# A two-block transformer kernel on one core: where the split of the next weight piece stands among the head steps of the gate tiles

## The chip, the cores and the metric

The kernel runs on one core of a Trainium2 chip. The metric is the device time of one execution in microseconds (us), of which less is better.

## What is computed

Two networks run one after the other on a sequence of 256 tokens of width 1024, in fp32. The first has two layers (windowed and neighbourhood attention with memory heads, gated feed-forward). The second, where the change lies, has one block:

```python
proj = jnp.dot(xn, w_in[l]) + b_in[l]
q, k, v, qi, ki, wi, xr, yr, gate_a, gate_b = jnp.split(proj, cuts, axis=-1)
attn = dsa_attention(...)            # 8 heads, keys chosen by a top-k of index scores
xr = causal_dwconv(xr, conv_rnn_w[l], conv_rnn_b[l])
rnn = rg_lru(xr, ...) * jax.nn.gelu(yr)
merged = (jax.nn.sigmoid(gate_a) * jnp.dot(attn, w_o_attn[l])
          + jax.nn.sigmoid(gate_b) * jnp.dot(rnn, w_o_rnn[l]))
h = h + ga1 * jnp.dot(merged, w_out[l])
```

## The kernel before

Every large product is done in three matmuls of type fp32r: activations and weights are each split into a high part (rounded to that type) and a low part (what is left), and high x high, high x low and low x high are summed in PSUM (L901 to L903). The weights come from memory in pieces of 128 partitions x 2048 numbers. For piece m, SP loads it into one of four raw buffers; ScalarE copies it to the high buffer `hi` (L1219), for which it waits until TensorE is done with piece m - 3 (`part_done`, three buffers); VectorE subtracts to get `lo` (L1663), and this subtraction lets TensorE use the piece and SP overwrite the raw buffer (the load of the piece four further on). These two instructions together are the step called the *split* of piece m.

The class `Order` writes one list of steps before the program is built, and each engine runs its own instructions of each step in the order of that list. So on every engine the order of the list is the order of the work, and an instruction that waits holds all that stands behind it on its engine. A *tile* of output columns (512 wide) takes two pieces, and the 24 matmuls of a piece are cut into two chunks of 12. `Order.part` (from L362) puts a chunk (`mm`), then, after a piece's first chunk, the split of the piece three further on, and between chunks it calls `between`, which takes the next entry of the tile's list in `IN2` (L35) or pops tasks that wait in `later`:

```python
            self.steps.append(("mm", m, ch))
            if ch == 0 and not self.hold:
                self.split_through(self.owed)
            if ch < p.chunks - 1:
                between()
```

The tiles of the second block's input projection are, in order: xr, qi, kvw, xr, yr, yr, q, then the two tiles of gate b (`gb`, pieces 112 to 115), the two of gate a (`ga`, 116 to 119), and then the recurrence's output projection (`orn`, 120 to 123). After them come `oat` (124, 125) and `out2`. In the gaps between their chunks stand, in order:

- gb: `gate1..` (the recurrence's two gates of half 1: TensorE matmuls, ScalarE Sigmoid L1343), `q0`, `q2` (transposes of q, split into parts), `top4` to `top7` (rounds of the top-k on VectorE), `rec1` (ScalarE: a table load, four Exp, four Tanh, two squares L1360; VectorE L1831); then `mask` (VectorE, L1820 to L1824), `inc1` (ScalarE square root, GpSimd product L1995), `attend`, `scan1` (VectorE scan L1837, then the GpSimd product L2000 that ends the recurrence of half 1).
- ga: `bias1` (GpSimd loads the bias rows of heads 4 to 7), `half1` (ScalarE L1368, VectorE L1842: the recurrence's output is split), and the head steps `att 0` to `att 5`.
- orn: the head steps 6 to 14.

A head step `att i` works on several heads at once (`attention` in each engine's program): TensorE transposes the weights of head i - 3 (called P below, L877), computes the scores of heads i and i + 1 if i is even, and multiplies the weights of head i - 5 with the values (L976 to L978). VectorE adds bias and mask to the scores of head i - 1 with their minimum (L1486), takes the reciprocal of the sum of head i - 2 (L1447), and makes the low part of P of head i - 4 (L1425). ScalarE makes the high part of that P (L1101) and the two exponentials of head i - 1 (L1125, L1126). GpSimd scales head i - 2 (L1901, L1902) and adds the mask for head i + 1 (L1884). At the end of a gate tile VectorE adds the bias to both halves (L1609).

Of the kernel before, what the change touches and what calls it, by code (L numbers as in the profile page):

```python
# [114 lines left out]
class Part:  # L115


    def __init__(self, m, at, tile, source, first, last, k0, nk, w):
        self.m, self.at, self.tile, self.source, self.first, self.last = m, at, tile, source, first, last
        self.k0, self.nk, self.w = k0, nk, w  # L120
        self.chunks = (2 * nk + 3) // 4
        if tile.bank:
            self.chunks = 2
# [13 lines left out]
class Order:  # L137
# [3 lines left out]
    def __init__(self, plan):  # L141
        self.plan = plan
        self.weights = [i for i, p in enumerate(plan) if p[0] != "ada"]
        self.steps, self.later, self.made = [], deque(), set()
        self.parts, self.tiles = [], []
        self.turn_n, self.turn_at, self.taken = 0, {}, {ON_A: 0, ON_D: 0}
        self.idle, self.tenant, self.bank_at, self.before = deque(range(8)), [None] * 8, {}, {}
        self.ada_at, self.split_next, self.owed, self.hold = {}, 0, 0, False
        self.squares, self.square_n = {}, 0
        self.h2_at, self.h2_n, self.silu_at, self.prod_at = {}, 0, {}, {}  # L150
        self.conv_at, self.conv_slots, self.pending, self.multiplied = {}, [], deque(), deque()
        self.tile_of = {}
        self.summed_by = {}
        self.res_at = {}
        self.run()
        self.count()
# [205 lines left out]
    def part(self, tile, source, first, last, between):  # L362
        m = len(self.parts)
        i = self.weights[m]
        _, k0, nk, w = self.plan[i][1]
        p = Part(m, i, tile, source, first, last, k0, nk, w)
        self.parts.append(p)
        for ch in range(p.chunks):
            for k in range(8) if tile.bank else [k0 + n % nk for n in range(4 * ch, min(4 * ch + 4, 2 * nk))]:
                self.need((source, k))  # L370
            self.steps.append(("mm", m, ch))
            if ch == 0 and not self.hold:
                self.split_through(self.owed)
            if ch < p.chunks - 1:
                between()
        self.owed = m + SPLITS
        if last:
            tile.m = m
            if tile.bank:
                self.turn_at[tile.bank] = (None, None, None)  # L380
# [122 lines left out]
    def run(self):  # L503
        for k in range(0, 8, 2):
            self.put("memx", k)
            self.split_through(min(k // 2, SPLITS - 1))
        self.later.extend([("rows",), ("relload",), ("xin", 0, 0), ("xin", 0, 2), ("xin", 0, 4), ("xin", 0, 6), ("memsq",), ("sq", 0, 0), ("sq", 0, 1)])
        self.linear("mem", 0, 0, 512, len(FIRST), "mem", [2, 1, 1, 2])
        self.mix(0)
        self.later.append(("rpb",))  # L510
        self.later.append(("small",))
        self.ffn(0)
        self.mix(1)
        self.drain()
        self.put("adaprep")
        self.ffn(1)
        self.drain()
        self.put("park")
        self.put("roots12")
        self.modulated(0)  # L520
        self.put("block2")
        for what, c, w, between in IN2:
            self.linear("yr" if what == "yr" else "in2", what, c, w, 1 if w <= 256 else 2, ("z", 0), 0, between)
        for c in (0, 512):
            self.linear("orn", 2, c, 512, 2, "r", 2)
        self.drain()
        self.put("fetch")
        self.put("sigmoid_a")
        for c in (0, 512):
            self.linear("oat", 2, c, 512, 1, ("y", 2))  # L530
        for c in (0, 512):
            self.linear("out2", 2, c, 512, 2, "merged")
        self.drain()
        self.put("root2")
        self.modulated(1)
        for c, w in UP2:
            for what in ("gate", "value"):
                self.linear("raw", what, c, w, 1, ("z", 1))
        self.later.extend([("flush",), ("flush",)])
        for c in (0, 512):  # L540
            self.linear("down2", 2, c, 512, 6, "h2")
        self.drain()
        self.put("root3")
        self.put("end")
# [1612 lines left out]
```

## Time and profile before

| what | us |
|---|---|
| runs, median of 3 | 1064.32 (1063.88 to 1067.81) |
| the profiled execution's own time | 1068.08 |
| its span, first to last instruction | 1066.0 |
| TensorE busy | 1014.6 (95%) |
| VectorE busy | 728.1 (68%) |
| ScalarE busy | 567.8 (53%) |
| GpSimd busy | 114.9 (11%) |
| mean granted TensorE clock | 0.988 |

How to read it: the page gives busy times and shares over the whole span; the trace below it gives single instructions with start and duration. The times in the trace count from the start of the span; the profiled execution's own time is 2.1 us longer than its span. The stage of the change lies between about 732 and 820 us. Of the chain of work that ended last, TensorE holds 73% and VectorE 10%.

### The profile page before, as it was taken

Reading aid. Unit: us, or ns where it says so; the run is one execution under the profiler, and the core shown is the slowest. Engines: PE = TensorE matmul, PEld = TensorE weight load, DVE = VectorE, ACT = ScalarE, POOL = GpSimd, SP = SyncE. Lnnn points to the kernel's source line nnn. Section 1 sums busy time; section 2 is a strip of 40 time slices with the busy share of each in tenths; the row PEclk is TensorE's granted clock in tenths of the full one; section 3 lists DMA queues with packets and bytes.
Section 4 is the critical chain, followed back from the end, with each engine's and each line's share of the span. In section 5 each row is a group of like instructions: output and inputs, shape, how many; then the busy total and the mean of one; then the engine's idle time right before and its main releaser. Section 6 shows DMA issues by size and latency. Waiting matters only on the chain.

```text
span 1066.0 us, 14098 instructions
## 1 busy us (share of the span) xinstructions
PE 1014.6 (95%) x5524; PEld 859.5 (81%) x5524; DVE 728.1 (68%) x984; ACT 567.8 (53%) x816; POOL 114.9 (11%) x167
## 2 busy tenths in 40 slices
PE   6998999999999989899999999999979999999996
PEld 5776777889888877788888877888867789999885
DVE  5668775566356568568878676688875767777753
ACT  6657654444345567544344435586656456565541
POOL 0112140000000022200000001122530000000001
PEclk9999999999999999999999998999999999999999
DMA  9765489655556431379999896555555436555541
GB/s 349 281 171 77 145 210 292 198 183 178 187 188 197 158 119 52 108 264 355 336 339 327 311 338 212 178 168 198 175 184 184 159 100 223 173 198 171 166 138 39
DMA packets 107376, 214.02 MB, mean 201 GB/s; under 512 B 4400, under 2 KB 32320, under 8 KB 103920
## 3 DMA queue, kind: packets, MB, share of 16 engines
q1 hardware_dynamic: 102640, 196.39, 54.5%
q0 software_dynamic: 4384, 16.51, 6.5%
q8 instruction: 44, 0.72, 0.3%
q10 hardware_dynamic: 288, 0.23, 0.1%
q14 instruction: 20, 0.16, 0.0%
HBM read 208.39 MB, written 6.15 MB: 201 GB/s over the span
## 4 chain that ended last, share of the span: by engine, by line
PE 73%; DVE 10%; ACT 7%; DMA 4%; issue 4%; POOL 1%; DVEq 0%; SPq 0%; ACTq 0%; POOLq 0%
PE bank L901 18%; PE bank L903 18%; PE bank L902 18%; PE bank L918 4%; PE bank L920 4%; PE bank L919 4%; ACT hi L1219 4%; DVE lo L1663 3%; PE bank L877 3%; DMA raw<-in_w_gate_up 3%; ACT junk L1089 1%; PE bank L930 1%; DMA raw<-in_w_in_a 1%; PE bank L879 1%; DVE early L1486 1%
## 5 line engine op out<-in xcount | busy, mean ns | idle before, releaser
L1663 DVE TENSOR_TENSOR lo<-raw,hi 128x2048 fp32r<-128x2048 f32 (+2 forms) x164 | 364.8, 2227 | 220.6 <-ACT hi L1219 220.2
L1219 ACT ACTIVATE hi<-raw 128x2048 fp32r<-128x2048 f32 (+2 forms) x164 | 303.6, 1855 | 243.3 <-PE bank L903 138.1
L901 PE MATMUL bank<-hi,xTh 128*128 128x512 f32 (+2 forms) x688 | 268.8, 391 | 1.2 <-DVE lo L1663 1.2
L903 PE MATMUL bank<-hi,xTl 128*128 128x512 f32 (+2 forms) x688 | 262.6, 382 | 0.0
L902 PE MATMUL bank<-lo,xTh 128*128 128x512 f32 (+2 forms) x688 | 262.2, 381 | 0.0
L901 PEld LDWEIGHTS bank<-hi,xTh 128*128 128x128 f32 x688 | 131.0, 190 | 26.1 <-DVE lo L1663 1.6
L903 PEld LDWEIGHTS bank<-hi,xTl 128*128 128x128 f32 x688 | 130.6, 190 | 25.2
L902 PEld LDWEIGHTS bank<-lo,xTh 128*128 128x128 f32 x688 | 130.9, 190 | 22.8
L901 PE MATMUL bank<-hi,hTh 128*128 128x512 f32 x264 | 103.3, 391 | 0.2 <-DVE lo L1663 0.2
L902 PE MATMUL bank<-lo,hTh 128*128 128x512 f32 x264 | 102.8, 389 | 0.0
L903 PE MATMUL bank<-hi,hTl 128*128 128x512 f32 x264 | 102.8, 389 | 0.0
L918 PE MATMUL bank<-xTh,hi 128*128 128x256 f32 x352 | 99.9, 284 | 1.7 <-DVE lo L1663 1.0
L919 PE MATMUL bank<-xTh,lo 128*128 128x256 f32 x352 | 99.6, 283 | 0.0
L920 PE MATMUL bank<-xTl,hi 128*128 128x256 f32 x352 | 99.6, 283 | 0.0
L918 PEld LDWEIGHTS bank<-xTh,hi 128*128 128x128 f32 x352 | 67.5, 192 | 2.3 <-DVE lo L1663 1.2
L919 PEld LDWEIGHTS bank<-xTh,lo 128*128 128x128 f32 x352 | 67.6, 192 | 0.0
L920 PEld LDWEIGHTS bank<-xTl,hi 128*128 128x128 f32 x352 | 67.6, 192 | 0.0
L901 PEld LDWEIGHTS bank<-hi,hTh 128*128 128x128 f32 x264 | 49.6, 188 | 10.7 <-DVE lo L1663 0.6
L903 PEld LDWEIGHTS bank<-hi,hTl 128*128 128x128 f32 x264 | 49.6, 188 | 10.3
L902 PEld LDWEIGHTS bank<-lo,hTh 128*128 128x128 f32 x264 | 49.6, 188 | 10.1
L1675 DVE SCALAR_TENSOR_TENSOR big<-raw,small,big 128x2048 f32<-128x2048 f32 x24 | 56.3, 2344 | 0.0
L1653 DVE SCALAR_TENSOR_TENSOR big<-bank,cols,big 128x255 f32<-128x255 f32 (+2 forms) x100 | 41.1, 473 | 3.4 <-ACT big L1325 2.8
(360 smaller groups left out, 1386.4 us busy)
## 6 DMA issues: line engine op xcount, KB each, us to landing
raw<-in_w_gate_up SPq DMA_DIRECT2D x44, 1024.0 KB, 7.2
raw<-in_w_down SPq DMA_DIRECT2D x30, 1024.0 KB, 5.1
raw<-in_w_ada SPq DMA_DIRECT2D x24, 1024.0 KB, 7.1
raw<-in_w_up SPq DMA_DIRECT2D x22, 1024.0 KB, 5.1
raw<-in_w_in SPq DMA_DIRECT2D x20, 1024.0 KB, 5.3
raw<-in_w_out SPq DMA_DIRECT2D x12, 1024.0 KB, 5.1
raw<-in_w_in_b SPq DMA_DIRECT2D x10, 1024.0 KB, 5.1
raw<-in_w_in_a SPq DMA_DIRECT2D x6, 1024.0 KB, 11.8
```

The lines of the kernel that those rows point to most:

```text
L877: e.transpose(bank[:, i * 128:(i + 1) * 128], x, ident)
L879: e.transpose(bank[:, n * 128:(n + 1) * 128], blocks[n], ident).then_inc(x_full, 1)
L901: e.matmul(o, sh, h[:, k, :], start=p.first and k == 0, stop=False)
L902: e.matmul(o, sh, lo[:, k, :], start=False, stop=False)
L903: done = e.matmul(o, sl, h[:, k, :], start=False, stop=p.last and k == p.nk - 1)
L918: e.matmul(o, h[:, k, at], xh[:, k, :], start=k == 0, stop=False)
L919: e.matmul(o, lo[:, k, at], xh[:, k, :], start=False, stop=False)
L920: done = e.matmul(o, h[:, k, at], xl[:, k, :], start=False, stop=k == 7)
L1219: e.activation(hi_s[m % SPLITS][:, 0:n], raw[p.at % RAWS][:, 0:n], ACT.Copy).then_inc(hi_made, 1)
L1653: e.scalar_tensor_tensor(out=o[:, j, n:], in0=bank[:, j * 256:j * 256 + 256 - n], scalar=weights[j][n - 1], in1=o[:, j, n:], op0=ALU.mult, ...
L1663: e.tensor_tensor(lo_s[s][:, 0:n], raw[p.at % RAWS][:, 0:n], hi_s[s][:, 0:n].bitcast(F), ALU.subtract).then_inc(lo_made, 1)
L1675: e.scalar_tensor_tensor(out=piece, in0=raw[i % RAWS][:, :], scalar=small[:, k:k + 1], in1=piece, op0=ALU.mult, op1=ALU.add).then_inc(ada_ ...
```

## The change

In the tiles of gate b and gate a, and in orn after them, a chunk's hook steps (what `between` puts) stand ahead of the split of the next piece, not behind it. The flag stays on through orn, since it is cleared only after that. Eleven splits move, those of pieces 114 to 124; the twelfth, of piece 125, keeps its place, as no step is left to pop there.

```diff
--- before.py
+++ after.py
@@ -151,6 +151,7 @@
         self.conv_at, self.conv_slots, self.pending, self.multiplied = {}, [], deque(), deque()
         self.tile_of = {}
         self.summed_by = {}
+        self.hooks_first = False
         self.res_at = {}
         self.run()
         self.count()
@@ -369,9 +370,12 @@
             for k in range(8) if tile.bank else [k0 + n % nk for n in range(4 * ch, min(4 * ch + 4, 2 * nk))]:
                 self.need((source, k))
             self.steps.append(("mm", m, ch))
+            first = self.hooks_first
+            if first and ch < p.chunks - 1:
+                between()
             if ch == 0 and not self.hold:
                 self.split_through(self.owed)
-            if ch < p.chunks - 1:
+            if not first and ch < p.chunks - 1:
                 between()
         self.owed = m + SPLITS
         if last:
@@ -520,10 +524,12 @@
         self.modulated(0)
         self.put("block2")
         for what, c, w, between in IN2:
+            self.hooks_first = what in ("gb", "ga")
             self.linear("yr" if what == "yr" else "in2", what, c, w, 1 if w <= 256 else 2, ("z", 0), 0, between)
         for c in (0, 512):
             self.linear("orn", 2, c, 512, 2, "r", 2)
         self.drain()
+        self.hooks_first = False
         self.put("fetch")
         self.put("sigmoid_a")
         for c in (0, 512):
```

Nothing changes on TensorE, GpSimd and SP. ScalarE around the step rec 1, before (`hi1<-raw3` is the high half of piece 115, `hi2<-raw0` of 116, `hi0<-raw1` of 117, `hi1<-raw2` of 118; the Exp write `nrm`, the Tanh `big`, the squares a bank; line numbers of the kernel before):

```order
L1219 ACTIVATE hi1<-raw3 128x2048 [waits part_done,d_raw3]
L1206 ACTIVATE q2yh<-bank1 128x512 [waits x_full]
L1353 ACT_TABLE_LOAD [waits x_act,rate_made]
L1353 ACTIVATE nrm<-big,small 128x256 [waits ig_x]
L1353 ACTIVATE nrm<-big,small 128x256 x3
L1357 ACTIVATE big<-big,small 128x256 [waits decay_made]
L1357 ACTIVATE big<-big,small 128x256 x3
L1360 ACTIVATE bank2<-nrm 128x512 [waits x_act]
L1360 ACTIVATE bank0<-nrm 128x512 [waits x_act]
L1219 ACTIVATE hi2<-raw0 128x2048 [waits part_done,d_raw0]
L1364 ACT_TABLE_LOAD
L1364 ACTIVATE big<-big 128x1024 [waits mult_made]
```

and in the changed kernel (its line numbers are higher by 6):

```order
L1212 ACTIVATE q2yh<-bank1 128x512 [waits x_full]
L1359 ACT_TABLE_LOAD [waits x_act,rate_made]
L1359 ACTIVATE nrm<-big,small 128x256 [waits ig_x]
L1359 ACTIVATE nrm<-big,small 128x256 x3
L1363 ACTIVATE big<-big,small 128x256 [waits decay_made]
L1363 ACTIVATE big<-big,small 128x256 x3
L1366 ACTIVATE bank2<-nrm 128x512 [waits x_act]
L1366 ACTIVATE bank0<-nrm 128x512 [waits x_act]
L1225 ACTIVATE hi1<-raw3 128x2048 [waits part_done,d_raw3]
L1370 ACT_TABLE_LOAD
L1370 ACTIVATE big<-big 128x1024 [waits mult_made]
L1225 ACTIVATE hi2<-raw0 128x2048 [waits part_done,d_raw0]
```

The high half of piece 115 has gone from ahead of the second copy of q to behind the squares.

VectorE around the head steps 2 and 3, before (`lo2<-raw3` is piece 119, `lo0<-raw0` piece 120; `ISA` rows are the scores of one head; `nrm<-` rows the bias adds of the gate tile):

```order
L1663 TENSOR_TENSOR lo2<-raw3,hi2 128x2048 [waits hi_made]
L1486 ISA acc,stat1<-bank0,big 128x128 [waits masked,p_made,x_full]
L1486 ISA stat1 128x1
L1486 ISA acc,stat1<-bank0,big 128x256
L1486 ISA stat1 128x1
L1447 RECIPROCAL stat0<-stat0 128x2 [waits exp_made]
L1609 TENSOR_TENSOR nrm<-bank3,gbc 128x512 [waits acc_first,d_brow1,r_low]
L1609 TENSOR_TENSOR nrm<-bank1,gbc 128x512 [waits part_done]
L1663 TENSOR_TENSOR lo0<-raw0,hi0 128x2048 [waits hi_made]
L1486 ISA stage0,stat2<-bank4,big 128x128 [waits masked,p_made,x_full]
L1486 ISA stat2 128x1
```

and in the changed kernel:

```order
L1492 ISA acc,stat1<-bank0,big 128x128 [waits masked,p_made,x_full]
L1492 ISA stat1 128x1
L1492 ISA acc,stat1<-bank0,big 128x256
L1492 ISA stat1 128x1
L1453 RECIPROCAL stat0<-stat0 128x2 [waits exp_made]
L1669 TENSOR_TENSOR lo2<-raw3,hi2 128x2048 [waits hi_made]
L1615 TENSOR_TENSOR nrm<-bank3,gbc 128x512 [waits acc_first,d_brow1,r_low]
L1615 TENSOR_TENSOR nrm<-bank1,gbc 128x512 [waits part_done]
L1492 ISA stage0,stat2<-bank4,big 128x128 [waits masked,p_made,x_full]
```

The scores of head 1 and the reciprocal of head 0 (`stat0`) are now ahead of piece 119's subtraction. Further on, the same kind of place between head steps 3 and 4, in the changed kernel:

```order
L1492 ISA stat2 128x1
L1453 RECIPROCAL stat1<-stat1 128x2 [waits exp_made]
L1669 TENSOR_TENSOR lo0<-raw0,hi0 128x2048 [waits hi_made]
L1492 ISA stage0,stat3<-bank5,big 128x128 [waits masked,p_made,x_full]
L1492 ISA stat3 128x1
L1492 ISA stage0,stat3<-bank5,big 128x256
L1492 ISA stat3 128x1
L1453 RECIPROCAL stat2<-stat2 128x2 [waits exp_made]
L1431 TENSOR_TENSOR p2l0<-bank2,p2h0 128x384 [waits x_high]
```

The subtraction of piece 120 now stands between the reciprocal of head 1 and the scores of head 3; before, it stood ahead of head 2's scores, and those of head 3 followed the reciprocal of head 1 directly.

## Rows read from the trace of the kernel before

**Rows 1.** The page: busy time of each engine, and the clock in 40 slices.
```profile
PE 1014.6 (95%) x5524; PEld 859.5 (81%) x5524; DVE 728.1 (68%) x984; ACT 567.8 (53%) x816; POOL 114.9 (11%) x167
...
PEclk9999999999999999999999998999999999999999
```

**Rows 2.** TensorE's timeline, 752 to 808: start us, us, line, operation, [idle before <- releaser].
```profile
752.18 0.39 PE L901 MATMUL bank<-hi,xTh 128*128 128x512 f32 x1
...
777.43 0.44 PE L877 MATMUL bank<-const 128*128 128x128 f32 x2 [3.81 <-POOL const L1902]
...
783.13 0.44 PE L877 MATMUL bank<-const,acc 128*128 128x128 f32 x2 [0.82 <-POOL acc L1902]
...
797.15 0.44 PE L877 MATMUL bank<-const 128*128 128x128 f32 x2 [1.32 <-POOL const L1902]
...
807.91 0.33 PE L976 MATMUL bank<-p2h,v2h 128*64 128x256 f32 x1 [1.50 <-DVE p2l L1425]
```

**Rows 3.** Windows: busy of each engine, then PEclk, DMA share, GB/s.
```profile
773.60:778.20 4.60, 0.79 (x6) 0.73 (x6) 4.04 (x8) 1.79 (x5) 1.64 (x4) 1.00 0.55 173
778.20:781.60 3.40, 3.40 (x10) 2.61 (x9) 2.37 (x2) 1.00 (x1) 0.29 (x1) 0.50 0.62 243
443.00:447.00 4.00, 3.76 (x14) 3.28 (x15) 1.91 (x5) 2.94 (x8) 0.00 (x0) 0.58 0.74 262
808.00:811.30 3.30, 3.30 (x19) 2.80 (x20) 1.75 (x4) 2.96 (x3) 0.00 (x0) 1.00 0.79 250
```

**Rows 4.** TensorE's timeline at 443, an earlier stage (transposes of the residual).
```profile
443.24 0.55 PE L877 MATMUL bank<-const,xres 128*128 128x128 f32 x3 [2.43 <-DVE xres L1529]
```

**Rows 5.** ScalarE's timeline, 741 to 751: pieces 115, 116, the step rec 1.
```profile
741.74 1.93 ACT L1219 ACTIVATE hi<-raw 128x2048 fp32r<-128x2048 f32 x1
...
744.79 1.28 ACT L1353 ACT_TABLE_LOAD   x1
...
749.44 1.10 ACT L1360 ACTIVATE bank<-nrm 128x512 f32<-128x512 f32 x2
750.48 1.90 ACT L1219 ACTIVATE hi<-raw 128x2048 fp32r<-128x2048 f32 x1
```

**Rows 6.** VectorE's timeline, 757 to 769: pieces 117, 118, scan, bias adds.
```profile
757.83 2.28 DVE L1663 TENSOR_TENSOR lo<-raw,hi 128x2048 fp32r<-128x2048 f32 x1
760.04 3.91 DVE L1837 TENSOR_TENSOR_SCAN big<-nrm,big 128x256 f32<-128x256 f32 x4
763.87 1.26 DVE L1609 TENSOR_TENSOR sgb<-bank,gbc 128x512 f32<-128x512 f32 x2
765.05 3.59 DVE L1663 TENSOR_TENSOR lo<-raw,hi 128x2048 fp32r<-128x2048 f32 x1
768.55 1.57 DVE L1842 TENSOR_TENSOR rTl<-nrm,keep 128x1024 fp32r<-128x1024 f32 x1
```

**Rows 7.** GpSimd's timeline at 764: the recurrence's product.
```profile
764.09 2.39 POOL L2000 TENSOR_TENSOR nrm<-nrm,big 128x1024 f32<-128x1024 f32 x1 [0.69 <-DVE big L1837]
```

**Rows 8.** VectorE's timeline, 773 to 777: piece 119, scores of head 1, reciprocal of head 0.
```profile
773.53 2.29 DVE L1663 TENSOR_TENSOR lo<-raw,hi 128x2048 fp32r<-128x2048 f32 x1 [2.86 <-ACT hi L1219]
775.74 0.28 DVE L1486 CUSTOM_DVE_ANT_0 acc<-bank,big 128x128 f32<-128x128 f32 x1
...
776.29 0.16 DVE L1447 RECIPROCAL stat<-stat 128x2 f32<-128x2 f32 x1
776.37 1.27 DVE L1609 TENSOR_TENSOR nrm<-bank,gbc 128x512 f32<-128x512 f32 x2
```

**Rows 9.** ScalarE's timeline, 770 to 778: exponentials of heads 0 and 1, piece 120.
```profile
770.71 0.40 ACT L1125 ACTIVATE const<-const,stat 128x128 f32<-128x128 f32 x1 [1.83 <-DVE stat L1486]
...
776.41 0.40 ACT L1125 ACTIVATE acc<-acc,stat 128x128 f32<-128x128 f32 x1 [2.91 <-DVE stat L1486]
...
777.30 1.90 ACT L1219 ACTIVATE hi<-raw 128x2048 fp32r<-128x2048 f32 x1
```

**Rows 10.** GpSimd's timeline at 776: head 0's weights are scaled.
```profile
776.56 0.37 POOL L1901 TENSOR_SCALAR const<-const,stat 128x128 f32<-128x128 f32 x1 [5.84 <-DVE stat L1447]
```

## The prediction

> **What bounds the kernel now.** The page comes first. Its busy line has TensorE at 95% of the span, VectorE at 68%, ScalarE at 53%, and the clock line has TensorE at full speed nearly everywhere [rows 1]. So time can be won or lost only where TensorE waits, or where its clock falls. TensorE's own timeline over the stage that the change touches (the two gate tiles, gb and ga, and the recurrence's output projection, orn) shows four waits: 3.81 us ahead of the transposes of head 0's weights (P0), 0.82 ahead of P1, 1.32 ahead of P4, and 1.50 ahead of the value matmuls of head 6 [rows 2]. They sum to 7.45 us. The windows show that for 3.4 us after the first wait the granted clock was 0.50, that is 1.2 GHz in place of 2.4 [rows 3]. Eight matmuls start there every 0.43 us in place of 0.227 us (the pace of the row at 752.18 and its successors), so 8 x 0.20 = 1.6 us are lost as well. The change can therefore win at most 7.45 + 1.6 = 9.05 us, 0.85% of 1068.08.
>
> Why does P0 wait? ScalarE had head 0's exponential at 770.71, but VectorE's reciprocal for it stands behind the low half of piece 119, which itself waited 2.86 us for ScalarE, and behind head 1's scores [rows 8]. The reciprocal started at 776.29; GpSimd scaled at 776.56 [rows 10], TensorE transposed at 777.43: 1.14 us from reciprocal to transposes. That is what a split in front of the head steps costs.
>
> **The change, part by part.** No instruction is added or removed, TensorE's order, GpSimd's and SP's are as before; eleven splits (pieces 114 to 124) each move on ScalarE (1.90 us [rows 5]) and VectorE (2.21 us from start to start [rows 6, 8]) behind the steps of one gap between chunks. I follow the engines from there. Prices from start to start: a head's two exponentials 0.89 (776.41 to 777.30 [rows 9]), scores into SBUF with reciprocal 0.63 (775.74 to 776.37), two bias adds 1.18 (763.87 to 765.05 [rows 6]). From the start of a head's scores step to the transposes that it releases are 0.55 + 1.14 = 1.69 us.
>
> Piece 114 moves behind four sigmoids, needs nothing, costs nothing: VectorE has it at 741.0, TensorE wants it at 746.7 (24 matmuls of 0.227 us ahead of 752.18).
>
> *Piece 115, the new wait.* It now stands behind the step rec 1 (table load, four Exp, four Tanh, two squares). These cannot start earlier than now, so ScalarE is free for the piece at 750.48, where piece 116's high half starts today, and not at 741.74 [rows 5]. High half to 752.4, low half to 754.7. TensorE wants the piece at 752.18 and starts at 754.75: **+2.55 us**. Queued behind it on VectorE are the bias adds and the top-k mask; the mask's second half ends with GpSimd's product at about 757.9 in both orders.
>
> *Piece 116* (behind mask, inc 1) takes the place of 117: 757.83 to 760.1 [rows 6]. TensorE, late by 2.55, wants it at 760.17: 0. *Piece 117* goes behind the scan, starts at 763.87 and is there at 766.1; wanted at 766.7: 0. But the row at 765.05 has such a subtraction in 3.59 us, ended 2.2 us after GpSimd's product (764.09 for 2.39 [rows 7]) was over: the two engines take turns. Now the subtraction is first by 0.2 us, so the product (and with it half 1 of the recurrence) is over at 768.5 and not at 766.5. Piece 118 follows to 770.7, the low half of the recurrence (1.5, the row at 768.55) to 772.2.
>
> *Head steps.* Head 0's scores step at 772.2, head 1's at 772.8, exponentials to 773.7 and 774.6, reciprocal at 773.8: P0 can be transposed at 774.9, TensorE arrives at 773.62 + 2.55 = 776.2. So the 3.81 us go, and with them the slow clock; P0 stands at **-1.2** against now. Then high half of 119 to 776.5, low to 778.75, bias adds to 779.95, head 2: P1 at 781.65, for which TensorE waits 2.2; against 783.13 that is **-1.5**. Now a loop shows that is not there today: exponentials of head 2 to 781.4, high half of 120 to 783.3, low half to 785.55, only then head 3's scores: P2 at 787.25, waited for 1.5, **-0.1** against its place now (787.36, right behind piece 119's first chunk). Then exponentials of head 3 (787.0), the copy of P1, head 4 (788.35), piece 121 to 792.5, bias adds to 793.7: P4 could go at 795.4, TensorE comes at 795.8, **-1.35** against 797.15. Heads 6 and 7: scores at 795.3, copies and exponentials to 797.5, piece 122 to 799.4 and 801.6, and P6, which hangs on head 7's step behind it, at 803.3. TensorE is there at 800.3 and **waits 3.0 us**. Now P6 starts at 801.71, so from there to the values of head 6 are 807.91 - 1.50 - 801.71 = 4.7 us of work, which gives 808.0; their operand is there at 805.7, so the 1.50 go: **+0.1**. After that every piece is early by over 1 us, and TensorE runs on.
>
> *The clock.* A wait of 3.0 us is new. The nearest rows: after 3.81 the clock fell; after 2.43 at 443.24 it fell too (0.58 over the next 4 us [rows 3, 4]); after the 1.50 at 807.91 it stayed at 1.00 [rows 3]. Ends: 0 and 1.6 us. 3.0 lies between two that fell, so I take **+1.6**. A fall after the waits at 754.75, 781.65 or 787.25 would be hidden mostly: TensorE waits again for VectorE's chain.
>
> The Trainium skill (TensorE: Matmul & The Clock Gate, Part 1) says that the activity monitor runs free of the kernel, so that the same kernel can pay in one run and not in another; by that the sum would be +0.1 in some executions and +1.7 in others. The two falls above agree that waits of this kind can cost; no row shows one that was spared.
>
> **Sum**: 0.1 + 1.6 = +1.7 us, 1068.08 to 1069.8 for the profiled execution. That execution lies 3.8 over the median of the runs, so the forecast for the median is 1064.32 + 1.7 = **1066.0**. In words: four waits of 7.45 become four of 2.55 + 2.2 + 1.5 + 3.0 = 9.25, in other places, and the slow stretch moves.
>
> DMA: loads are released by a piece's low half. Piece 119's waits for 115's, late by 8.5 us now (754.7, not 746.2), lands some 5 us later at 760, and is read at 774.6. Piece 126's is issued at 801.4 and read near 822. On GpSimd's queue the bias rows of heads 4 to 7 follow the product 2 us later, are there by 776, and serve masks that head 4's scores want after 787. Price 0.
>
> **The rivals.**
> *All head waits go* (faster). Were the chain of exponential, split, scores as short as TensorE's chunk (12 x 0.227 = 2.7 us) plus its small matmuls, only the wait for piece 115 would stay: -9.05 + 2.55 = -6.5, so 1057.8. For it: P0's wait surely goes. Against it: exponential, both halves and scores make 0.89 + 1.90 + 2.21 + 0.63 = 5.6 us per loop, and loops at P1 and P6 hold more than one head. It decides if VectorE reaches the head steps 3 us earlier than I have it. Chance 0.11.
> *The clock falls after each new wait and nothing is absorbed* (slower). Place: TensorE after the waits at 754.75, 781.65, 787.25 and 803.3. Price: 9.25 - 9.05 + 4 x 1.6 = +6.6, so 1070.9. For it: a wait of 2.43 was enough once. Against it: 1.50 was not, and VectorE's chain, which sets P1 and P2, does not start later when TensorE is slower. It decides if waits under 2 us are enough, and if bias adds, which wait for TensorE, pass its delays to the chain. Chance 0.12.
> *Piece 115 costs nothing*, since some of rec 1 starts earlier without the split ahead of it: TensorE reaches each later place 2.55 earlier, but P1, P2 and P6 hang on VectorE, so the sum lies 0.2 to 1.7 lower: 1064.3 to 1065.8, inside no change.
>
> **How the numbers follow.** A measurement of this kernel can tell about 0.5% (5.3 us) from no change. Forecast with its neighbour 0.76 (nearly all inside 0.5%), faster rival 0.11, slower rival 0.12, the rest in both tails. Hence faster 0.12, same 0.75, slower 0.13. The forecast's own range is 1062.9 (no fall, P6 earlier by 1.5) to 1067.6 (a second fall that is not absorbed). The range goes on to the slower rival, and half way to the faster: 1060.5 to 1071.0.
>
> **What would show it.** Right: a TensorE wait of some 2.5 us for the low half at 752; no wait at P0 and clock 1.00 there; waits of 1.5 to 3 at P1, P2 and P6; VectorE's subtraction ahead of GpSimd's product at 764; the value matmuls of head 6 without a wait; a slow clock after P6. Wrong: no wait at 752, or P6 on time (then faster by more), or TensorE in the oat tiles over 4 us later than now (then the chain of splits and heads is longer than worked out).

## The result, and the profile after

The changed kernel took 1071.13 us (median of 10 runs, 1068.55 to 1074.33), the kernel before 1067.3 us (median of 10 runs, the three that the forecast started from among them, 1063.88 to 1069.27): **ratio 1.0037, 95% interval 1.0025 to 1.0048**, slower by 3.8 us. That is inside the 0.5% called no change, as forecast, but by twice the forecast +1.7 us. 1071.13 lies just over the range's end of 1071.0; the kernel before itself came out 3 us above the 1064.32 that the forecast started from, so only the ratio tells the size of the effect. Of the 5.1 us between the forecast's 1066.0 and 1071.13, 3.0 are that starting value and 2.1 are the change.

The profiled execution took 1070.77 us, 2.7 over that of before. The top of its page answers to [rows 1]:

```profile
span 1068.8 us, 14098 instructions
...
PE 1014.6 (95%) x5524; PEld 859.5 (80%) x5524; DVE 729.0 (68%) x984; ACT 567.2 (53%) x816; POOL 116.7 (11%) x167
...
PEclk9999999999999999999999999999999999999999
```

TensorE's work is the same; so the difference is waits and clock. TensorE's timeline from 750 to 810 (start us, us, line, operation, [idle before <- releaser]), all waits over 0.4 us, answers to [rows 2]:

```profile
753.86 0.50 PE L907 MATMUL bank<-hi,xTh 128*128 128x512 f32 x1 [2.42 <-DVE lo L1669]
...
760.88 0.50 PE L907 MATMUL bank<-hi,xTh 128*128 128x512 f32 x1 [1.28 <-DVE lo L1669]
...
782.12 0.44 PE L883 MATMUL bank<-const,acc 128*128 128x128 f32 x2 [2.03 <-POOL acc L1908]
...
804.38 0.65 PE L883 MATMUL bank<-const,stage 128*128 128x128 f32 x2 [3.46 <-POOL stage L1908]
```

The waits for pieces 115 and 116, for P1 and P6. None stands any more at P0, at P4 or ahead of the value matmuls of head 6. The sum is 9.19 us; before it was 7.45.

The windows after the first, third and fourth wait (busy of each engine, PEclk, DMA share, GB/s) answer to [rows 3]:

```profile
753.90:757.30 3.40, 3.40 (x15) 2.83 (x16) 3.40 (x6) 3.40 (x2) 1.98 (x2) 1.00 0.70 217
784.00:787.40 3.40, 3.40 (x9) 2.63 (x9) 3.40 (x8) 0.86 (x4) 0.46 (x2) 0.50 0.02 2
804.40:807.80 3.40, 3.40 (x13) 3.02 (x14) 2.10 (x5) 1.45 (x4) 1.36 (x3) 0.51 1.02 368
```

The clock held at 1.00 after 2.42 us of waiting; after P1 and after P6 it fell to 0.50 and 0.51, that is 1.2 GHz.

To compare executions that do not reach this stage at the same moment, I count from the start of ScalarE's first copy of q, ahead of the step rec 1, and end at the first `hi<-hi,keep` matmul of orn's second tile, behind the last wait. ScalarE's timeline before:

```profile
741.26 0.60 ACT L1206 ACTIVATE q2yh<-bank 128x512 fp32r<-128x512 f32 x1
```

and after:

```profile
740.36 0.60 ACT L1212 ACTIVATE q2yh<-bank 128x512 fp32r<-128x512 f32 x1
```

The stage ends at 836.62 before and at 839.24 after. So it grew from 95.36 to 98.88 us, by 3.5, and the changed kernel had come to it 0.9 us earlier; that lead is not the change's doing (the last section has where such differences come from). The table counts every place from this start. "Forecast" is the prediction's own time minus 741.26.

| place | before | forecast | after | after minus forecast |
|---|---|---|---|---|
| piece 115 | 10.92 | 13.49 | 13.50 | 0.0 |
| P1 | 41.87 | 40.39 | 41.76 | +1.4 |
| P2 | 46.10 | 45.99 | 47.57 | +1.6 |
| P6 | 60.45 | 62.04 | 64.02 | +2.0 |
| end of stage | 95.36 | 97.1 | 98.88 | +1.8 |

Piece 115 came to 0.01 us where it was forecast. Between it and P1 1.4 us came in that the prediction does not have, and the next TensorE wait there is the one for piece 116, which was costed at 0. What held it up stands on GpSimd's timeline, 755 to 765 of the changed kernel:

```profile
755.31 0.59 POOL L1898 DMA_DIRECT2D gbc<-in_b_in  x1 [12.36 <-DVE sgb L1615]
755.91 2.41 POOL L2001 TENSOR_TENSOR big<-big 128x1024 f32<-128x1024 f32 x1
758.77 5.33 POOL L1890 TENSOR_TENSOR big<-big,left 128x128 f32<-128x128 f32 x4 [0.44 <-DVE left L1830]
764.79 4.31 POOL L2006 TENSOR_TENSOR nrm<-nrm,big 128x1024 f32<-128x1024 f32 x1 [0.69 <-DVE big L1843]
```

and before:

```profile
752.93 0.59 POOL L1892 DMA_DIRECT2D gbc<-in_b_in  x1 [9.06 <-DVE sgb L1609]
754.91 2.52 POOL L1995 TENSOR_TENSOR big<-big 128x1024 f32<-128x1024 f32 x1 [1.38 <-ACT big L1364]
```

The issue of a bias row's load stands in GpSimd's queue ahead of its product in inc 1, and waits for the bias additions of tile 4424 on VectorE, because these read the buffer that it fills. Before, the additions were done in time: the issue was over 1.38 us before ScalarE had the product's operand. Now the additions stand behind piece 115's late subtraction, the issue is released at 755.31, and the product starts behind it, 1.9 us later in the stage (15.55 against 13.65). VectorE's timeline shows who pays:

```profile
751.51 2.29 DVE L1669 TENSOR_TENSOR lo<-raw,hi 128x2048 fp32r<-128x2048 f32 x1 [0.98 <-ACT hi L1225]
753.72 1.28 DVE L1615 TENSOR_TENSOR sgb<-bank,gbc 128x512 f32<-128x512 f32 x2
754.92 0.42 DVE L1826 TENSOR_SCALAR acc<-left 128x128 f32<-128x128 f32 x2
755.25 3.36 DVE L1830 SCALAR_TENSOR_TENSOR left<-acc,const 128x128 f32<-128x128 f32 x2
758.54 2.28 DVE L1669 TENSOR_TENSOR lo<-raw,hi 128x2048 fp32r<-128x2048 f32 x1
```

The mask (L1830) takes 3.36 us for two small operations (0.62 in `c_115` below), whose second half ends with GpSimd's product, and piece 116's subtraction stands behind it. All that VectorE does later is later by as much.

### The profile page after: what moved, and what is told of

It is laid out like the page before. It is cut to its first block, busy times and chain, and to the rows that moved or that the text cites. A ratio compares the mean times of both kernels' runs of the same rounds, so it can differ in the third digit from the quotient of the medians.

```text
span 1068.8 us, 14098 instructions
## 1 busy us (share of the span) xinstructions
PE 1014.6 (95%) x5524; PEld 859.5 (80%) x5524; DVE 729.0 (68%) x984; ACT 567.2 (53%) x816; POOL 116.7 (11%) x167
## 4 chain that ended last, share of the span: by engine, by line
PE 73%; DVE 10%; ACT 7%; DMA 4%; issue 4%; POOL 1%; SPq 0%; DVEq 0%; ACTq 0%; POOLq 0%
PE bank L907 18%; PE bank L909 18%; PE bank L908 18%; ACT hi L1225 4%; PE bank L924 4%; PE bank L925 4%; PE bank L926 4%; DVE lo L1669 4%; PE bank L883 3%; DMA raw<-in_w_gate_up 3%; PE bank L936 1%; ACT junk L1095 1%; DMA raw<-in_w_in_a 1%; PE bank L885 1%; DVE early L1492 1%
```

## The experiments

Eleven kernels, each with the same work in another order. Where a kernel starts from the changed one, its diff is against that.

### The change in gate b alone, and in gate a and orn alone

`a_gb` keeps the new order for pieces 114 to 117 only:

```diff
-            self.hooks_first = what in ("gb", "ga")
+            self.hooks_first = what == "gb"
...
+        self.hooks_first = False
         for c in (0, 512):
             self.linear("orn", 2, c, 512, 2, "r", 2)
```

> Only the tiles of gate b have the splits (pieces 114 to 117) behind their hook steps; gate a and orn are as before. Theory T (the cost of the change comes from gate b, where pieces 115 and 116 come late and push VectorE's chain back by some 3.5 us; in gate a and orn waits are only exchanged): 3 to 4 us over the kernel before (1.003 to 1.004), TensorE waits of about 2.4 us for piece 115 and 1.3 for 116, and the wait of P0 is back at 3 to 4 us with the slow clock behind it. Rival R (the loops of exponential, split and scores in gate a and orn, with the waits at P1 and P6, are the cost): 0 to 1 us over before.

`a_ga_orn` keeps it for pieces 118 to 124:

```diff
-            self.hooks_first = what in ("gb", "ga")
+            self.hooks_first = what == "ga"
```

> Only gate a and orn (pieces 118 to 124) have the splits behind the hook steps; gate b is as before. T: -0.5 to +0.5 us against the kernel before (0.9995 to 1.0005): no wait for pieces 115 and 116, none at P0, but about 2.6 us at P1, 1.5 at P2 and 3.0 or a little more at P6. R: +3 us (1.003).

Measured: `a_gb` ratio 1.0032 (1.0019 to 1.0045), stage 101.75 us, +6.4 against before. `a_ga_orn` ratio 0.9991 (0.9983 to 1.0000), stage 95.24 us, -0.1. TensorE's timeline of `a_ga_orn`, its three waits in the stage:

```profile
778.60 0.44 PE L883 MATMUL bank<-const,acc 128*128 128x128 f32 x2 [2.81 <-POOL acc L1908]
...
784.30 0.44 PE L883 MATMUL bank<-const,stage 128*128 128x128 f32 x2 [1.31 <-POOL stage L1908]
...
800.81 0.44 PE L883 MATMUL bank<-const,stage 128*128 128x128 f32 x2 [3.48 <-POOL stage L1908]
```

Moving the head steps ahead exchanges waits of 7.45 us for others of 7.60, and P6 stands at 60.45, where it stood before. The whole cost comes from gate b: there the head steps gain nothing from the new order, since there are none, and pieces 115 and 116 come late. In `a_gb` the old order of gate a then gives P0 a wait of 2.98 us, P1 one of 2.39 and slow clocks behind 115 and P1 (0.60 and 0.50). The wait for piece 116 that was expected there does not show: TensorE comes to it at the slow clock. The profiled execution, at 1072.72 us, was the longest of six, and its stage shows +6.4 us where the medians show +3.4; the stage of one profile is not the kernel's mean.

### The bias row's issue behind the product

`a_row` is the changed kernel, with one DMA issue of GpSimd moved behind the product of inc 1:

```diff
-                        bias_row(row_no[t_.c] + 2)
+                        if t_.c != 4424:
+                            bias_row(row_no[t_.c] + 2)
...
+                    if half == 1:
+                        bias_row(row_no[4424] + 2)
```

> The changed kernel, but GpSimd issues the load of the bias row that waits for the bias adds of the first gate b tile behind its product of the step inc 1, not ahead of it. If that issue of 0.6 us and its wait push the product, the mask and with them piece 116 (theory T1), the wait of 1.28 us for piece 116 goes and the time falls by 1 to 1.4 us against the changed kernel (+2.5 against before). Rival: the mask waits for ScalarE's square root and the product whatever stands ahead, and nothing changes (+3.7 against before).

Measured: ratio 1.0007 (0.9993 to 1.0021), stage 97.42 us, 1.46 less than in the changed kernel. GpSimd's timeline:

```profile
753.59 2.41 POOL L2002 TENSOR_TENSOR big<-big 128x1024 f32<-128x1024 f32 x1 [11.04 <-ACT big L1370]
755.95 0.59 POOL L1898 DMA_DIRECT2D gbc<-in_b_in  x1
```

and TensorE's:

```profile
753.45 0.50 PE L907 MATMUL bank<-hi,xTh 128*128 128x512 f32 x1 [2.42 <-DVE lo L1669]
...
780.34 0.44 PE L883 MATMUL bank<-const,acc 128*128 128x128 f32 x2 [2.04 <-POOL acc L1908]
...
786.04 0.44 PE L883 MATMUL bank<-const,stage 128*128 128x128 f32 x2 [1.32 <-POOL stage L1908]
...
802.56 0.44 PE L883 MATMUL bank<-const,stage 128*128 128x128 f32 x2 [3.47 <-POOL stage L1908]
```

The product now waits for ScalarE alone and starts at 13.64 of the stage (15.55 in the changed kernel), which rules out the rival; the wait for piece 116 is gone, and the stage (start at 739.95) has P1 at 40.39, P2 at 46.09, P6 at 62.61. These are the forecast's own places (40.39, 45.99, 62.04), with its four waits: 2.55, 2.2, 1.5 and 3.0 forecast, 2.42, 2.04, 1.32 and 3.47 measured. So this kernel is what the prediction described, and its stage is +2.1 us against before where +1.7 was forecast. A 0.59 us issue in the wrong place of a queue is the rest. By the medians the move is worth 3.2 us (1.0037 to 1.0007, each uncertain by 0.0011 to 0.0014), by the stage 1.5; the two agree within that.

### Piece 115 in its old place

`c_115`, the changed kernel but for the first of the moved splits that cost something. (The split of piece 115 stands behind the first chunk of piece 113: `owed` is set a piece earlier, so the split is that of the piece two further on, not three as the section on the kernel before has it.)

```diff
-            first = self.hooks_first
+            first = self.hooks_first and m != 113
```

> The changed kernel, but piece 115 keeps its old place ahead of q2, top and rec 1. T (VectorE's chain through mask, scan and recurrence sets the end, not TensorE's own wait): the wait of 2.4 us for piece 115 goes, a wait of about 2.5 us for piece 116 comes in its place, and the time falls by only 1 to 1.4 us against the changed kernel, by way of the earlier bias adds. Rival R2 (TensorE's wait for piece 115 is carried through to the end): 2.4 us or more less than the changed kernel.

Measured: ratio 0.9999 (0.9987 to 1.0011), stage 94.39 us, 4.5 less than in the changed kernel and 1.0 less than before. The wait at 115 is gone and comes back one piece later, as expected:

```profile
761.00 0.79 PE L907 MATMUL bank<-hi,xTh 128*128 128x512 f32 x1 [2.60 <-DVE lo L1669]
...
786.48 0.44 PE L883 MATMUL bank<-const,stage 128*128 128x128 f32 x2 [0.75 <-POOL stage L1908]
...
803.01 0.44 PE L883 MATMUL bank<-const,stage 128*128 128x128 f32 x2 [3.49 <-POOL stage L1908]
```

The size was not as expected: 4.1 us by the medians (1.0037 to 0.9999), where T had 1 to 1.4 and only R2 had 2.4 or more. Yet R2's mechanism is not what the rows show, since the wait of 2.60 us stands at piece 116. P6 stands at 61.13, 2.9 us earlier than in the changed kernel. VectorE's rows in `c_115` and then the scan in the changed kernel show where that comes from:

```profile
755.38 5.57 DVE L1669 TENSOR_TENSOR lo<-raw,hi 128x2048 fp32r<-128x2048 f32 x1 [1.25 <-ACT hi L1225]
760.87 2.42 DVE L1843 TENSOR_TENSOR_SCAN big<-nrm,big 128x256 f32<-128x256 f32 x4
```

```profile
760.74 3.91 DVE L1843 TENSOR_TENSOR_SCAN big<-nrm,big 128x256 f32<-128x256 f32 x4
```

Piece 116's subtraction ends 1.4 us earlier in the stage than in the changed kernel (19.1 against 20.5), which is what T counted. It took 5.57 us where it takes 2.28 elsewhere: GpSimd was in its product from 754.17, went on to the mask's four operations at 756.54 and ended them at 758.79, and the subtraction ended 2.2 us after that. By then GpSimd was done, and the scan took 2.42 us; in the changed kernel GpSimd's same four operations (758.77, 5.33 us in all) overlap the subtraction and the scan, and the scan took 3.91. That is the other 1.5 us. So the two engines hold each other up here too, as the forecast had it at 764, and the order in which they meet has a price.

The rest of the stage's 4.5 us is the clock, which stayed at 1.00 behind P6 (the window 803.00 to 806.40). From P6 to the end of the stage this kernel needs 33.26 us, the changed kernel 34.86 with its clock at 0.51: 1.6 us is what that fall costs, the forecast's price for it. The wait ahead of it was 3.49 us here and 3.46 there, so that the clock held in one and fell in the other is not the change's doing.

### Only the subtraction late: a version that should beat both

The experiments so far say that head steps ahead of a split help P0, and that ScalarE's high half behind them hurts, since VectorE's subtraction then waits for it (2.52 and 2.78 us of VectorE's idle time at 777.03 and 783.92 of the changed kernel). `b_low` is the kernel before, in which in gate a and orn only VectorE's subtraction goes behind the hook steps, ScalarE's half stays ahead:

```diff
+                if self.late_low:
+                    self.lows.append(m)
+                else:
+                    self.steps.append(("low", m))
...
+            while self.lows:
+                self.steps.append(("low", self.lows.pop(0)))
```

> The kernel before, but in gate a and orn ScalarE's high half of a split stays ahead of the head step and only VectorE's subtraction goes behind it (pieces 118 to 124). If what costs in both orders is that VectorE stands idle for the high half (2.86, 1.60, 2.12 us before; 2.52, 2.78, 2.13, 1.95 in the changed kernel) while head steps are queued behind it (theory T2), those idle times shrink to under 1 us, the waits at P0 and P6 go, P1 keeps about 1.7 us, and the stage is 5 to 7 us shorter: 0.993 to 0.996. Rival R3 (VectorE's own work, not its idling, paces the head steps): -1 us, as with gate a and orn alone.

`b_low_mix` does so in the tiles of mix(0) and mix(1) as well, `b_low_all` everywhere.

> b_low, and the same order in the attention stages of the first network's two layers, where TensorE waits about 5 and 4 us in all for GpSimd's scaled weights. T2: another 2 to 5 us less than b_low. R3: the same as b_low.

> The high half ahead and the subtraction behind the hook steps everywhere. T2: gate b gets a wait of about 1.4 us for piece 115 (its subtraction behind rec 1), elsewhere little changes: 1 to 3 us more than b_low_mix. R3: near the kernel before plus 2 us.

Measured: `b_low` 0.9981 (0.9968 to 0.9994), stage 93.09 us; `b_low_mix` 0.9955 (0.9939 to 0.9971), stage 94.00, so its gain on `b_low` does not lie in the stage, to which it comes 0.95 us earlier; `b_low_all` 1.0060 (1.0041 to 1.0080), which has waits of 1.35 and 1.28 for pieces 115 and 116 in gate b and is 3.5 us behind already at 87 us. A late subtraction did not pay outside the head steps.

T2 came out in half. Of VectorE's idle times for a high half, one of 1.64 us is left and the others are gone, and P0 waits no more; but P6 still waits 1.54 us, and the stage is 2.3 us shorter and not 5 to 7. P1 waits longer than in any kernel above:

```profile
779.83 0.44 PE L886 MATMUL bank<-const,acc 128*128 128x128 f32 x2 [4.14 <-POOL acc L1911]
```

Its releaser is GpSimd's scaling. GpSimd's timeline at 777:

```profile
777.00 2.33 POOL L1910 TENSOR_SCALAR acc<-acc,stat 128x128 f32<-128x128 f32 x1 [4.08 <-DVE stat L1456]
779.30 0.47 POOL L1911 TENSOR_SCALAR acc<-acc,stat 128x256 f32<-128x256 f32 x1
```

and VectorE's:

```profile
776.74 0.16 DVE L1456 RECIPROCAL stat<-stat 128x2 f32<-128x2 f32 x1
776.82 2.27 DVE L1672 TENSOR_TENSOR lo<-raw,hi 128x2048 fp32r<-128x2048 f32 x1
```

The scaling took 2.33 us where that of head 0 took 0.37 before [rows 10]: the subtraction started 0.18 us ahead of it and ran for 2.27, and the scaling ended 0.24 us after it. The Trainium skill (SBUF — State Buffer, "SBUF: two separate sides") says that VectorE and GpSimd share a pair of ports under an exclusive lock, which a VectorE operation with two inputs in SBUF takes against a GpSimd operation that reads SBUF, and that whoever starts first keeps it for the whole instruction. The lengths of such rows agree: 2.33 for 0.37 here, 5.57 for 2.28 in `c_115`, 4.31 for 2.39 at 764.79 of the changed kernel and, right behind it, 3.29 for 2.28 (piece 118's subtraction at 767.95). The kernel puts this subtraction straight behind the reciprocal that releases GpSimd.

### Away from the reciprocal

If that is so, something else must stand between the reciprocal and the subtraction. `d_mix_rcp` is `b_low_mix` with the reciprocal of a head ahead of the next head's scores, not behind them, in this stage; `d_rcp` does only that to the kernel before; `d_mix_rcp_all` does it in all attention stages.

```diff
-                if 0 <= i - 1 < n:
+                first = stage == 2
+                if not first and 0 <= i - 1 < n:
...
+                if first and 0 <= i - 1 < n:
+                    soften(stage, i - 1)
```

> b_low_mix, and in the head steps of the second network VectorE takes the reciprocal of head i - 2 before the scores of head i - 1, not behind them. Theory T3 (in b_low TensorE waits 4.14 us at P1 because the subtraction of piece 120 starts 0.08 us behind the reciprocal and holds GpSimd's scaling for its 2.3 us): the scaling starts ahead of the subtraction, GpSimd's 2.33 us row falls to 0.37, the wait at P1 falls to 1.5 us or less, and the time by about 2.5 us against b_low_mix (0.993). Rival: the scaling is slow for another reason, and only the 0.5 us of the order are won.

> The kernel before, with the reciprocal ahead of the scores in the second network's head steps alone; the splits stay ahead of the head steps. There the reciprocal stands behind a subtraction and its wait for the high half, not ahead of one: T3 gives only the 0.5 us per chain (P0, P1, P4), 0 to 1.5 us less than before.

> The same, with the reciprocal first in the head steps of all three stages. Where a head's exponential is not ready, the reciprocal now holds the next head's scores. T3: 0 to 2 us less than d_mix_rcp, since TensorE waits for scaled weights in the first two stages too. Rival: as much more, since the reciprocal waits for the exponential there.

Measured: `d_mix_rcp` 0.9959 (0.9943 to 0.9974), stage 92.24, by the ratio no gain on `b_low_mix`; `d_rcp` 0.9978 (0.9962 to 0.9994), stage 94.56, which is 0.8 us less as expected, while the ratio says 2.4; `d_mix_rcp_all` 1.0000 (0.9983 to 1.0018), stage 93.82, but it reaches the stage at 741.98, 2.6 us later than `d_mix_rcp`. That does not come from longer waits, as the rival had it: up to 446 us TensorE waits 28.2 us in all in this kernel and 27.9 in `d_mix_rcp`. But its clock stands at 0.91 in the windows 20 to 40 and 80 to 100, where that of `d_mix_rcp` is 1.00, and its executions lie at mean clocks of 0.979 to 0.990 (`d_mix_rcp` 0.986 to 0.990). Whether the order brings the falls on was not tried. The wait at P1 went from 4.14 to 3.76 only. GpSimd's timeline of `d_mix_rcp` says why:

```profile
775.63 0.38 POOL L1917 TENSOR_SCALAR acc<-acc,stat 128x128 f32<-128x128 f32 x1 [3.52 <-DVE stat L1461]
775.98 2.59 POOL L1918 TENSOR_SCALAR acc<-acc,stat 128x256 f32<-128x256 f32 x1
```

and VectorE's:

```profile
775.38 0.15 DVE L1461 RECIPROCAL stat<-stat 128x2 f32<-128x2 f32 x1
775.45 0.27 DVE L1502 CUSTOM_DVE_ANT_0 stage<-bank,big 128x128 f32<-128x128 f32 x1
...
775.99 2.31 DVE L1679 TENSOR_TENSOR lo<-raw,hi 128x2048 fp32r<-128x2048 f32 x1
```

The scores cover the first scaling (0.38), but GpSimd has a second one, and it met the subtraction: 2.59 in place of 0.47. By these rows the scaling started 0.01 us ahead of the subtraction and was held up all the same, so they don't show that the first to start keeps the ports; a start is not resolved so finely here. The head start that the scores give is 0.6 us; the two scalings need 0.85 and start 0.25 behind the reciprocal. In this the expectation (P1 at 1.5 us or less, 0.993) was wrong, the mechanism was not.

### The bias additions in between

`e_adds` is `d_mix_rcp` with VectorE's two bias additions of the ga tile 3400, which read a bank, put between that reciprocal and the subtraction:

```diff
+            while self.adds and ch < p.chunks - 1:
+                self.steps.append(("adds", self.adds.pop(0)))
...
+        if t.l == "ga" and t.c == 3400:
+            self.adds.append(t.j)
...
-                elif kind == "evac":
+                elif kind == "adds" or (kind == "evac" and (tiles[name[0]].l, tiles[name[0]].c) != ("ga", 3400)):
```

> The kernel before with the late subtraction in gate a's tiles, in mix(0) and mix(1), and with the reciprocal first in stage 2 (as in the run d_mix_rcp); new: the bias additions of the ga tile stand on VectorE behind head step 3, ahead of the subtraction for chunk 120, so that additions that read a bank (1.2 us each) and not the subtraction of 2.3 us stand behind the reciprocal of head 1. T3 (what keeps head 1's scaling late is a VectorE subtraction with two inputs in SBUF that starts just ahead of GpSimd's scaling and holds it up for its whole length): GpSimd's two scalings of head 1 take 0.37 and 0.47 us, TensorE's wait at P1 falls from 3.76 us to 1 us or less, the stage is about 3 us shorter than in d_mix_rcp, ratio 0.993. Rival (the lock only moves again, or the subtraction for chunk 120, now later, takes the time back as a wait of TensorE for piece 120, or the bank that the additions free late is missed): ratio as d_mix_rcp, 0.996.

Measured: **1058.16 us (median of 6 runs; the kernel before beside it 1067.94), ratio 0.9914 (0.9891 to 0.9936)**. VectorE's timeline:

```profile
771.85 0.15 DVE L1465 RECIPROCAL stat<-stat 128x2 f32<-128x2 f32 x1
...
772.46 1.28 DVE L1629 TENSOR_TENSOR nrm<-bank,gbc 128x512 f32<-128x512 f32 x2
773.66 2.52 DVE L1683 TENSOR_TENSOR lo<-raw,hi 128x2048 fp32r<-128x2048 f32 x1
```

GpSimd's:

```profile
772.10 0.38 POOL L1921 TENSOR_SCALAR acc<-acc,stat 128x128 f32<-128x128 f32 x1 [2.32 <-DVE stat L1465]
772.45 0.48 POOL L1922 TENSOR_SCALAR acc<-acc,stat 128x256 f32<-128x256 f32 x1
```

TensorE's:

```profile
772.99 0.44 PE L894 MATMUL bank<-const,acc 128*128 128x128 f32 x2 [0.45 <-POOL acc L1922]
...
774.03 0.33 PE L947 MATMUL bank<-k2Th,q2yh 64*128 64x128 f32 x2 [0.49 <-DVE nrm L1629]
...
791.78 0.44 PE L894 MATMUL bank<-const,stage 128*128 128x128 f32 x2 [1.00 <-POOL stage L1922]
```

Both scalings run at full pace, P1 waits 0.45 us in place of 3.76, and the additions cost TensorE 0.49 in turn. All waits of the stage are 1.94 us, the clock is 1.00 behind each of them (windows 769 to 781 and 791 to 795), and the stage is 87.98 us, 4.3 less than in `d_mix_rcp` (the ratios differ by 0.45%, 4.8 us). The rival's number, 0.996, is out. This kernel beats both.

Not all of that is the lock. In `d_mix_rcp` the additions stood ahead of the reciprocal of head 1 (at 774.18, the reciprocal at 775.38), so moving them lets the reciprocal start 1.2 us earlier in the stage (34.75 against 35.95), whatever GpSimd does. The second scaling ends 3.3 us earlier (35.8 against 39.1): 1.2 by that, 2.1 by its full pace. No kernel has the one without the other. And of the stage's 4.3 us the waits make 2.8 (1.94 in place of 4.75); about 1.5 are the clock, which was at 0.67 behind P1 in `d_mix_rcp`. The profiled execution, 1056.3 us, was the shortest of its six.

## Why the prediction came out as it did

- **Piece 115, +2.55**: right. It started at 13.50 against 13.49, with a wait of 2.42. ScalarE began the high half at 749.58, behind the squares, at 9.22 of the stage, as worked out.
- **Piece 116, "TensorE, late by 2.55, wants it at 760.17: 0"**: this is the step that failed. The step before it had it wrong already: "the mask's second half ends with GpSimd's product at about 757.9 in both orders". The product did not stay. The prediction names what is queued behind piece 115's subtraction on VectorE, the bias additions first, but does not ask who waits for those. A bias row's issue does, on GpSimd, and the product stands behind it. The prediction looked at that very queue for heads 4 to 7 and priced it at 0, and missed its first entry. `a_row` took that entry away and got the forecast's places to 0.1 us at P1 and P2, 0.6 at P6. The cost was 1.46 us of the stage.
- **Piece 117 and the lock**: the mechanism was right, and the way round too: VectorE's subtraction came first (764.57) and GpSimd's product took 4.31 us in place of 2.39 [rows 7]. Relative to the start the product ended 1.5 us later than forecast (28.7 against 27.2), which is piece 116's delay passed on.
- **P0, P1, P2, P4**: no wait at P0 and none at P4, right. P1's wait 2.2 forecast, 2.03 measured. P2's 1.5 was not seen in the changed kernel, because TensorE came there at the slow clock; in `a_row`, where the clock held, it was 1.32.
- **P6, 3.0**: 3.46 and 3.47 in both kernels. Of the +2.0 us at P6, 1.4 are piece 116's; the other 0.6 is a chain of copies and exponentials a little longer than summed. The 1.50 ahead of head 6's values are gone, as forecast.
- **The clock**: +1.6 after P6, right in this execution (0.51; 1.6 us by `c_115`), but in part by luck: `c_115` waited 3.49 us at the same place and its clock stayed at 1.00. That a length between two that fell must fall too does not hold. "A fall after the waits at 754.75, 781.65 or 787.25 would be hidden mostly": right as well. It fell after P1, but from P1 to P6 the changed kernel needs 22.26 us and `a_row`, with its clock at 1.00 behind P1 (780.40 to 783.80), 22.22.
- **The sum**: forecast +1.7, with piece 116 it would have been +3.2; the stage shows +3.5, the medians +3.8.
- **The starting value**: the prediction took the profiled execution, 1068.08, as 3.8 us over the kernel's median, by three runs. Ten runs have the median at 1067.3, so it was 0.8 over, and 3.0 of the 5.1 us by which 1066.0 missed come from that step.
- **The rivals**: "all head waits go" failed where the prediction said it would, at the loops of P1 and P6. "The clock falls after each wait and nothing is absorbed", +6.6, was too much by the absorbing.

The better question the experiments put is why the gain of P0's 3.81 us bought nothing. Both orders put a whole split between head steps, and the order only chooses which of two heads waits. With the subtraction alone put late, the wait that was left was another one, of GpSimd held up by that subtraction; with other work between the reciprocal and the subtraction the stage is 7.4 us shorter than before. 5.5 us of these are waits (1.94 in place of 7.45); most of the rest is the slow clock behind P0, 1.6 by the prediction's count, which this execution did not have.

## What to carry to other kernels

When an instruction is made later, follow not only what stands behind it on its own engine but, one step on, who on another in-order queue waits for those, and what stands behind that waiter: a 0.59 us DMA issue on GpSimd passed a delay on to a product, a mask and two transposes. When two engines block each other, look at what each starts straight after the instruction that releases the other, and put there something that does not take part, for long enough to cover all that the other has to do. Here the bias additions, which read a bank, ran beside the scalings (0.38 and 0.48). One input in SBUF is not a safe sign by itself: in `a_row` a VectorE operation of that kind (`acc<-left` 128x128, L1826) took 1.57 us beside GpSimd's product, and 0.22 without it in the changed kernel. Count stages from a common event in both traces; it showed 0.01 us agreement where the run times showed 3 us of scatter. And look at the clock in both before calling a difference of stages the order's.

## What the runs showed of the hardware

The clock does not fall by the length of a wait alone. The prediction inferred from falls after 2.43 and 3.81 us [rows 2, 3, 4] that 3.0 us would do too. The same transposes at the same place wait 2.43 to 2.45 us in these kernels. Windows of 4 us from there, for the changed kernel:

```profile
444.10:448.10 4.00, 4.00 (x22) 3.46 (x23) 1.98 (x6) 3.27 (x9) 0.00 (x0) 1.00 0.62 246
```

for `d_mix_rcp`:

```profile
440.70:444.70 4.00, 4.00 (x16) 3.31 (x17) 1.99 (x6) 3.31 (x9) 0.00 (x0) 0.65 0.61 248
```

and for `e_adds`:

```profile
440.70:444.70 4.00, 4.00 (x22) 3.47 (x23) 1.99 (x6) 3.34 (x9) 0.00 (x0) 1.00 0.61 244
```

In 4 us the first and third run 22 matmuls, the second 16. In the kernel before the clock fell there (0.58), in the changed kernel it did not. At these transposes the changed kernel is 0.84 us behind (444.08 against 443.24), at the start of the stage 0.90 ahead: 1.7 us, the price of about one fall. Likewise the wait at P6 left the clock at 1.00 in `c_115` (3.49 us) and at 0.51 in the changed kernel (3.46). The 2.42 us ahead of piece 115 left the clock at 1.00 in the changed kernel and in `a_row`, and at 0.60 in `a_gb`; 2.03 and 2.04 at P1 gave 0.50 and 1.00. The Trainium skill (TensorE: Matmul & The Clock Gate, Part 1) says that the gate's activity window runs free of the kernel, so that the warm-up of one kernel differs from run to run. These rows agree so far that both outcomes follow waits of one length; they are single executions of different kernels. A single profile can thus be off by 1.6 us for each wait of 2 us or more, and a difference of that size between two profiles needs either several runs or a count from a common event. That the falls are also what spreads the run times of one kernel (1063.71 to 1071.83 us in one set of the kernel before) was not tried, but the mean clocks of its runs point that way: of the 30 beside `a_gb`, the nine at 0.986 took 1069.65 us on average, the four at 0.990 took 1067.87.
